# Norm weights and token factors moved from the normed tile to the copies out of PSUM, in a two-layer pooling, attention and expert kernel

## The reference, cut to what matters

```python
def rms_norm(x, g, eps=RMS_EPS):
    y = x * lax.rsqrt(jnp.mean(x * x, axis=-1, keepdims=True) + eps)
    return y * g

for i in range(2):
    h = rms_norm(x, norm_mix_g[i])
    x = x + (pool_mixer(h, pool_w, pool_scale) if i == 0 else diff_attention(h, wq, wk, wv, wo, ...))
    h = rms_norm(x, norm_ffn_g[i])
    x = x + hier_moe(h, ...)      # sum over two experts e of gate_e * ((silu(h @ w1[e]) * (h @ w3[e])) @ w2[e])
return rms_norm(x, final_g)
```

## Time and profile before

| | |
|---|---|
| median of 3 runs | 1154.34 us (1152.5 to 1156.3) |
| the profiled execution itself | 1155.02 us |
| its span | 1153.2 us |
| busy PE / PEld / DVE / ACT | 869.2 / 504.9 / 350.0 / 216.3 us |
| bytes moved by DMA | 427.74 MB |
| mean granted TensorE clock | 0.918 of full speed |
| chain that ended last | PE 43%, DMA 38%, DVE 9%, issue 7%, ACT 2% |

### The profile page before, as it was taken

The page is one execution under the profiler, slowest core; times in us unless marked ns, Lnnn a source line. Parts: engine busy times, 40 slices in busy tenths (PEclk is TensorE's granted clock), DMA queues, the critical chain, the costliest instruction groups (busy, mean ns, idle before and its releaser), DMA issues.

```text
span 1153.2 us, 19469 instructions
## 1 busy us (share of the span) xinstructions
PE 869.2 (75%) x7944; PEld 504.9 (44%) x7945; DVE 350.0 (30%) x815; ACT 216.3 (19%) x487; POOL 5.1 (0%) x15
## 2 busy tenths in 40 slices
PE   6978676667675687678999997888786666676865
PEld 4654334333443343344787564454443333333432
DVE  3533222221322222223156442331232222222223
ACT  3312112110111111111145212210111111101112
POOL 1000000000000000000000000000000000000000
PEclk9899899988998888888999989998898999889988
DMA  9989999999999999997403449999999999999992
GB/s 312 404 351 425 425 422 426 426 426 422 425 427 425 422 427 423 426 428 296 184 1 145 172 160 427 424 425 423 426 425 425 422 426 426 428 424 423 427 393 93
DMA packets 33196, 427.74 MB, mean 371 GB/s; under 512 B 4292, under 2 KB 5572, under 8 KB 7704
## 3 DMA queue, kind: packets, MB, share of 16 engines
q1 hardware_dynamic: 32600, 424.18, 87.4%
q0 software_dynamic: 448, 1.25, 0.5%
HBM read 424.37 MB, written 1.05 MB: 369 GB/s over the span
## 4 chain that ended last, share of the span: by engine, by line
PE 43%; DMA 38%; DVE 9%; issue 7%; ACT 2%; DVEq 0%; SPq 0%; ACTq 0%
DMA ring<-in_moe_w 38%; PE ps L426 15%; PE ps L462 7%; PE ps L595 5%; PE ps L477 4%; DVE work L1017 3%; PE ps L581 3%; PE ps L393 3%; PE ps L649 2%; DVE work L1025 1%; ACT work L725 1%; PE ps L379 1%; DVE hT L1051 1%; DVE work L1019 1%; DVE work L1021 1%
## 5 line engine op out<-in xcount | busy, mean ns | idle before, releaser
L426 PE MATMUL ps<-ring,work 128*32 128x256 f32 x4224 | 304.0, 439 | 193.7 <-DMA ring<-in_moe_w 114.2
L426 PEld LDWEIGHTS ps<-ring,work 128*32 128x32 f32 x4224 | 163.7, 125 | 335.1 <-issue 249.2
L1015 DVE TENSOR_SCALAR work<-work 128x128 f32<-128x128 f32 (+1 forms) x64 | 14.7, 229 | 493.3 <-ACT work L725 493.3
L393 PE MATMUL ps<-work,h_sb 128*128 128x256 f32 x576 | 150.6, 409 | 12.5 <-issue 11.8
L462 PE MATMUL ps<-ring,work 128*32 128x256 f32 x2112 | 131.3, 384 | 27.1 <-DVE work L1025 25.9
L1051 DVE COPY hT<-ps 32x512 f32<-32x512 f32 x128 | 87.4, 683 | 160.6 <-PE ps L462 159.7
L393 PEld LDWEIGHTS ps<-work,h_sb 128*128 128x128 f32 x576 | 110.1, 201 | 55.6 <-issue 42.2
L725 ACT ACTIVATE work<-ps 128x256 f32<-128x256 f32 x64 | 24.5, 383 | 502.3 <-PE ps L426 502.3
L462 PEld LDWEIGHTS ps<-ring,work 128*32 128x32 f32 x2112 | 62.8, 110 | 94.0 <-DVE work L1025 47.6
L733 ACT COPY hT<-ps 32x512 f32<-32x512 f32 x128 | 73.9, 577 | 135.7 <-PE ps L462 135.0
L477 PE MATMUL ps<-hT,work 128*128 128x512 f32 x136 | 62.6, 605 | 12.1 <-DVE hT L1051 12.1
(11 more groups left out here) (146 smaller groups left out, 421.5 us busy)
## 6 DMA issues: line engine op xcount, KB each, us to landing
ring<-in_moe_w SPq DMA_DIRECT2D x192, 2048.0 KB, 30.4
ring<-in_attn_wv SPq DMA_DIRECT2D x2, 2048.0 KB, 32.2
ring<-in_attn_wq SPq DMA_DIRECT2D x2, 2048.0 KB, 32.7
ring<-in_attn_wk SPq DMA_DIRECT2D x2, 2048.0 KB, 33.1
ring<-in_attn_wo SPq DMA_DIRECT2D x2, 2048.0 KB, 35.7
x_sb<-in_x SPq DMA_DIRECT2D x2, 512.0 KB, 6.4
work<-in_pool_w SPq DMA_DIRECT2D x1, 1024.0 KB, 13.0
out_x<-h_sb SPq DMA_DIRECT2D x2, 512.0 KB, 3.3
```

The costliest lines, as they stand in the source:

```text
L393: mm = pe.matmul(xg_ps(bank)[:, q, :], h_sb[:, t, kt * P:(kt + 1) * P], onehot[:, u, t].rearrange("p b e s -> p (b e s)"), start=(t == 0), ...
L426: mm = pe.matmul(gu_ps[SB * j:SB * (j + 1), b, :, :], xg[:, u, kt, b, k, :], w[:, :, kt, P * j:P * (j + 1)], start=(kt == 0 and b == 0), s ...
```

## The change: what it does

- h_sb, gain and root no longer stand between x and the transposes. PE transposes x_sb itself, reading every eighth element, as soon as x is there (s_x2).
- The gain of a norm, now as columns (gcol, features on partitions), multiplies in copy_hT: ACT does four products of 128x128 with a scale per partition, DVE one product with a broadcast operand. In the experts the gain comes with the copy of the gathered tokens, now two instructions of 128x256 where one of 128x512 stood.
- The root for attention: v is multiplied by it in its copies; q and k, whose tokens lie along the free axis, are multiplied by rrow, a row that PE makes by a product of ones with a diagonal matrix that DVE writes from the root. DVE now does the q and k copy, as one product of 128x512; ACT did two of 128x256.
- normalise_tokens writes h_sb permuted from x_sb times the root.
- ACT's order changes: copy_hT comes ahead of norm. In layer 0 both halves are transposed before the first router product, and both token factors come after both copies.
- Three column loads of gcol stand in SP's queue after the constants; two row loads and two broadcasts are gone. POOL's load of the second ffn gain is gone, and the one of final_g waits for s_x2 at 4.
- Three banks are cleared before the ranks and one after them, which takes the place of the extra product.
- PE's spare passes move out of experts. After layer 0 PE runs second_layer as the body of a condition "at most 64 tokens", and the spare passes with a second copy of second_layer stand in its else part; after layer 1 a branch over the spare passes stays.

```diff
-            for r, g in enumerate((norm_mix_g[0:1, :], pool_scale[0:1, :], norm_ffn_g[0:1, :], norm_mix_g[1:2, :])):
+            for r, g in enumerate((norm_mix_g[0:1, :], pool_scale[0:1, :])):
...
             sp.dma_start(cst[:, :], consts[:, 0:C_BAND]).then_inc(s_c, 16)
+            for i, g in enumerate((norm_mix_g[1, :], norm_ffn_g[0, :], norm_ffn_g[1, :])):
+                sp.dma_start(gcol[:, i, :], g.rearrange("(p k) -> p k", k=KT)).then_inc(gcol_in, 16)
...
-            def transposes(count, t):
-                pe.wait_ge(s_h, 2 * count + t + 1)
+            def transposes(number, t):
+                pe.wait_ge(s_x2, 2 * number + t + 1)
                 for k in range(KT):
                     mm = pe.transpose(ps[:, 2 * t + k // 4, (k % 4) * P:(k % 4 + 1) * P],
-                                      h_sb[:, t, k * P:(k + 1) * P], ident)
+                                      x_sb[:, t, :].rearrange("p (q k) -> p k q", k=KT)[:, k, :], ident)
...
+                if layer == 0:
+                    for t in range(TH):
+                        transposes(number, t)
                 for t in range(TH):
-                    if t > 0 and layer == 0:
-                        pe.wait_ge(s_bcc, 3)
-                    if t > 0 or layer == 0:
-                        transposes(2 * layer + 1, t)
-                    if t == 0 and layer == 0:
-                        pe.wait_ge(s_bcc, 2)
-                        broadcast(3, 2)
+                    if t > 0 and layer == 1:
+                        transposes(number, t)
...
-                for b in range(ACC):
-                    pe.matmul(ps[:, b, :], zero, cst[:, 0:512], start=True, stop=True)
+                for b in range(1, ACC):
+                    clear(b)
                 pe.wait_ge(s_A, layer + 1)
...
-                keep_clock(FILL_RANKS, 0)
+                clear(0)
...
                 if t == 1:
-                    broadcast(2, 2)
                     pe.wait_ge(s_bcc, 1)
...
+            def second_layer():
+                transposes(1, 0)
...
+                pe.wait_ge(s_diag, 1)
+                for t in range(TH):
+                    mm = pe.matmul(ps[:, 4, t * P:(t + 1) * P], ones, diag[:, t, :], start=True, stop=True)
+                mm.then_inc(s_rr, 1)
...
+                route(1, 2)
+                experts(1)
+                most = pe.value_load(cnt[0:1, NE + NGRP:NE + NGRP + 1], min_val=0, max_val=S)
+                with pe.If(most > CAP):
+                    passes(1, most)
+
+            most = pe.value_load(cnt[0:1, NE + NGRP:NE + NGRP + 1], min_val=0, max_val=S)
+            with pe.If(most < CAP + 1):
+                second_layer()
+            with pe.Else():
+                passes(0, most)
+                second_layer()
...
             def copy_hT(number, t):
                 act_e.wait_ge(s_tr, 4 * number + 2 * t + 1)
-                act_e.copy(hT[:, 0:4, t * P:(t + 1) * P], ps[:, 2 * t, :].rearrange("p (k s) -> p k s", k=4))\
-                     .then_inc(s_hT[1], 1)
+                for k in range(4):
+                    ins = act_e.mul(hT[:, k, t * P:(t + 1) * P], ps[:, 2 * t, k * P:(k + 1) * P], hT_gain(number)[:, k:k + 1])
+                ins.then_inc(s_hT[1], 1)
...
-                act_e.copy(xg[:, u, KPR * r:KPR * (r + 1)].rearrange("p k b e s -> p k (b e s)"), xg_ps(bank)).then_inc(s["xgc"], 1)
+                for q in range(KPR):
+                    kt = KPR * r + q
+                    ins = act_e.mul(xg[:, u, kt].rearrange("p b e s -> p (b e s)"), xg_ps(bank)[:, q, :],
+                                    gcol[:, 1 + layer, kt:kt + 1])
+                ins.then_inc(s["xgc"], 1)
...
-                act_e.mul(h_sb[:, t, :], h_sb[:, t, :], root_x[:, t:t + 1]).then_inc(s_hn, 1)
+                act_e.mul(h_sb[:, t, :].rearrange("p (k q) -> p k q", k=KT),
+                          x_sb[:, t, :].rearrange("p (q k) -> p k q", k=KT), root_x[:, t:t + 1]).then_inc(s_hn, 1)
...
-            def copy_queries_keys(h):
-                act_e.wait_ge(s_q, h + 1)
-                act_e.mul(qT[:, h, :], ps[:, h % 2, 0:S], HD ** -0.5)
-                act_e.copy(kT[:, h, :], ps[:, h % 2, S:2 * S]).then_inc(s_qc, 1)
...
             for t in range(TH):
+                copy_hT(2, t)
                 norm(3, t, work[:, 4096:4096 + D])
-                copy_hT(2, t)
                 normalise_tokens(1, t)
...
+            def copy_hT(number, t):
+                ve.wait_ge(s_tr, 4 * number + 2 * t + 2)
+                ve.tensor_tensor(hT[:, 4:8, t * P:(t + 1) * P], ps[:, 2 * t + 1, :].rearrange("p (k s) -> p k s", k=4),
+                                 hT_gain(number)[:, 4:8].unsqueeze(2).to_broadcast([P, 4, P]), ALU.mult).then_inc(s_hT[0], 1)
+
+            def token_factor(count, t):
+                root(count, t)
                 ve.sem_inc(s_r, 1)
...
             for t in range(TH):
                 residual(t, main["sc"], ACC * (NGRP - 1))
-                norm(2, t, gain[:, 0, :], True)
                 copy_hT(1, t)
+                token_factor(2, t)
+                ins = ve.tensor_scalar(diag[:, t, :], ident, root_x[:, t:t + 1], None, ALU.mult)
+            ins.then_inc(s_diag, 1)
...
+            def copy_queries_keys(h):
+                ve.wait_ge(s_q, h + 1)
+                ve.tensor_tensor(qk[:, :, h, :], ps[:, h % 2, :].rearrange("p (m s) -> p m s", m=2), rrow[:, :, :], ALU.mult)\
+                  .then_inc(s_qc, 1)
...
             for t in range(TH):
                 residual(t, s_wo, 0)
-                router_norm(3, t, gain[:, 1, :])
                 copy_hT(2, t)
+                token_factor(3, t)
```

More of the change, by code:

```diff
@@ L64 @@
 C_ALL = C_BAND + len(WINDOWS) * BW
-FILL_RANKS, FILL_LAST = 1, 1
+FILL_LAST = 1
 def shape_constants():
@@ L107, in build @@
         hT = sb("hT", [P, KT, S])
-        gain = sb("gain", [P, 2, D])
+        gain = sb("gain", [P, D])
+        gcol = sb("gcol", [P, 3, KT])
+        rrow = sb("rrow", [P, 2, S])
         cst = sb("cst", [P, C_BAND])
@@ L563, in _ @@
             experts(0)
-            transposes(2, 0)
-            u = CPE * NE // RING + 1
-            def matrix(c, kt):
-                return ring[:, c + kt // 4, :].rearrange("p (k n) -> p k n", k=4)[:, kt % 4, :]
-            for t in range(TH):
-                wait_hT(1, t)
-                for kt in range(KT):
-                    if t == 0 and kt % 4 == 0:
-                        pe.wait_ge(loaded[kt // 4], 16 * u)
-                    if t == 0 and kt == KT - 2:
-                        transposes(2, 1)
-                    for i in range(2):
-                        mm = pe.matmul(ps[:, 2 * t + i, :], hT[:, kt, t * P:(t + 1) * P],
-                                       matrix(0, kt)[:, 512 * i:512 * (i + 1)], start=(kt == 0), stop=(kt == KT - 1))
-                mm.then_inc(s_vp, 1)
@@ L1175, in normalise @@
                 ins.then_inc(s_os, 1)
-            for h in range(1, NH + 3):
-                if h <= NH:
+            for h in range(NH + 3):
+                if h < NH:
+                    copy_queries_keys(h)
+                if 1 <= h <= NH:
                     logits(h - 1)
```

310 lines of the change are left out of this document (154 added, 156 removed).

## The result

The kernel after takes **1139.08 us** (median of 4 runs, 1138.26 to 1141.13) against 1154.48 (4 runs, 1152.5 to 1156.3) of the kernel before on the same chip: ratio 0.987, 95% interval 0.985 to 0.989. It is faster by 15.4 us. The profiled execution took 1139.63 us for a span of 1137.8; the one before had 1155.02 for 1153.2, so the two spans differ by 15.4 as well and can be taken apart.

What follows compares the result with a forecast made beforehand. It took the weight stream as the bound in the expert loops and PE in attention; 3.2 + (4.3 + 2.7 - 0.45) + 1.7 - 2.8 = 8.65 us off the median 1154.34 gave 1145.6, range 1140.5 to 1151.5.

Steps and rivals of the forecast that it cites:

- the 2.8 us that it charged for PE's strided reads: Transposes' weight loads at v and layer 1's routing: 0.09 us more per load by DVE's factor 1.56, four sets of 8.
- The head: Start of the kernel, up to the weight stream's restart: the stream runs on 3.2 us earlier (1.0 to 5.1).
- The two waits side by side: Before the transposes between the layers: norm and PE's far branch, branch ending last by 0.5 us; removing both gains 4.3.
- The rival of a clock that stays low: At the v product between the layers: PE's clock stays low, gain 6.0 us, time 1148.3; chance 0.25.
- the branch that is only moved: Between the layers: new condition still jumps, transposes start at 522.9 as before; gain 1.6 us, 1152.7; chance 0.08.
- the rival with 0.25: Transposes' strided weight loads on PE are free: gain 11.5 us, time 1142.8; chance 0.25.
- The standstill: At the head: ring full at about 56.3 us, DMA engines start again at about 62.1, 5.8 us of standstill.
- The queued residual: Layer 1's routing: DVE's second-half residual queues behind its wait for the factor, ending at 662.1 instead of 660.46.
- the router product starts at 664.0 instead of 664.46: Layer 1's routing, after DVE's second-half residual; with the moved clear, 1.7 us together.
- The clear moved behind the ranks: Layer 1's routing: one clear of four moves behind the ranks; with the earlier router product, ranks at 672.6, 1.7 us together.
- under the stream, 0: Expert loops: 72 copies of gathered tokens become 144, about 0.1 us more each, hidden under the weight stream.
- The end and the attention loop: End: one more jump on PE, 0, at worst 0.1 us; attention: DVE takes q and k copies, 0.7 us each, cost 0.

Runs made afterwards that it cites:

- the four kernels: Kernel before; it with only PE's spare passes set aside, 1152.08 us; kernel after with them back behind the loop, 1150.54; kernel after.
- first pair: First profiled executions of the kernels before and after, cut into stretches at the same events; differences sum to 15.4 us.
- gcol_pool: Kernel after with the three column loads of the norm weights issued by POOL instead of SP: 1139.72 us.
- second pair: Both kernels, unchanged, profiled again: before 1156.34 us, after 1139.88; the differences of their stretches sum to 15.7 us.
- single edits: Kernel before with only PE's spare passes set aside, 1152.08 us; kernel after with the spare passes back behind the loop, 1150.54 us.

## Why the prediction was right, and where it was not

The forecast failed by two terms of its sum: the 2.8 us that it charged for PE's strided reads, which measured 0.02 us for each set of 8, and the 0 that it put for layer 1's expert loop, which gained 3.2. With these two as measured its sum of 8.65 would be 14.65, and the time 1139.7. The head was underrated by 1.2 to 2.0 us as well, and the routing overrated.

*Between the layers: right.* The two waits side by side, the mechanism on which the forecast rested, are what the four kernels show. The way from the scatter's end to v shrank by 4.5 us in the first pair and 4.9 in the second (4.3 was put, less 0.7 for strides), and v by 2.0 to 2.6 (2.7 for the clock, less 0.45, less 0.7). The rival of a clock that stays low is out at v, where the first 24 records took 10.54 us, and so is the branch that is only moved: 80 ns. A low clock behind a short idle did occur at layer 1's second router product, which took 3.48 us behind 0.87 us of idle time, as before the change.

*Strided reads: wrong, the step from the load to the path.* DVE's factor of 1.56 was carried to PE's weight load and every load was charged in full, -2.8 us. Measured: the load record grew by 0.05 us where 0.09 was put, and the pace of transposes by 0.002, 0.07 us for 32. The overlap was what the sum had left out. This was the rival with 0.25, and with it alone the time would have been 1142.8, which is inside the range and still 3.7 us too high.

*The head: right in kind, 3.2 for a measured 4.4 to 5.2.* Two terms of the sum were off. The ring was put 2.6 us later by three issues at 1.05 each; it started 0.7 later. The router products were put at 3.63 us for each half, 7.3 in all, the price at the low clock; all 32 records took 5.98, so the logits came 4.6 us sooner, not 3.0. The standstill went nearly whole, and gcol_pool shows no more to win there.

*Layer 1's routing: wrong.* 1.7 was put, and 0.3 after the strides; the pairs show 1.4 and -0.4, which is the clock's scatter. The queued residual was found as predicted. But the step "the router product starts at 664.0 instead of 664.46" named DVE as what comes last, and costed ACT's strided scaling as hidden behind it, at 0.6 more where it is 1.0. As soon as DVE is relieved ACT ends the wait, at the same instant. The clear moved behind the ranks gained only in the execution that the rows are from, where the clears ran at the low clock.

*The expert loops: wrong, the step "under the stream, 0".* The work inside the loop is hidden, as said; the loop's own code was not looked at. Layer 1's stream is 3.2 to 3.3 us shorter. This is half of the miss of 6.5 us, and the only part that no rival named. The split copies were put at 0.1 us more each; a pair takes 0.94 us for 0.59, hidden as forecast.

*The end and the attention loop: right.* DVE's eight products take 692 ns each and attention stays at 103.6 us; the far jump ends before the span does.

The terms again, forecast to measured: 3.2 to 4.4, 3.6 to 4.5, 1.55 to 2.0 (with 0.5 lost ahead of the scatter in the first pair), 0.3 to 1.4 or -0.4, 0 to 3.2, 0 to 0.4. The first four stand for the head, the way to v, v and the routing; then come layer 1's stream and the end. In the second pair the end is 0.9 us longer, so only the head, the way to v, v and the stream were underrated beyond what two executions differ by.

## What to carry to other kernels

Where two waits end within half a microsecond of each other, price them as a pair. Here neither edit alone shortened the way from the scatter's end to v (6.1 and 7.1 us for 6.2 or 6.6), and both together took it to 1.7 and left v's start at full clock. Read what a single edit gains by stretches, too: the 2.8 and 4.4 us of the single edits came from other places. Before charging an access pattern, measure it on the engine that will do it, and at the pace of a row of such instructions: one instruction's record can grow without costing anything. And do not read a 1.4 us gain out of a single profile. In the stretches in which TensorE ran at either clock two executions of the same kernel differed by up to 1.9 us (last gate product to v, before), while attention and the way from layer 1's first gather to its exponential came back within 0.1 in both kernels, and v in the kernel after.

## What the runs showed of the hardware

- Instructions on their way to the engines are traffic on the DMA engines: 23 further packets of about 8 KB on the queue of an idle engine lengthened a stretch of 439 us of weights by 5.9 us, 8 packets by nothing. They delayed one of the 16 parts in which a load lands, by 0.5 to 0.7 us each, and no other part.
- The 16 parts of one 2 MB load drift apart in a saturated stream: about 2 us from first to last at 36 us into layer 1's stream, and at its end eight parts land about 10 us ahead of the other eight. The last part sets when the chunk can be used, and the stream's last 10 us run at about half rate.
- Moving PE's code by 64 instructions changed its waits for instructions in the expert loops from 79.5 to 63.4 us and layer 1's stream by 1.5 to 1.9 us, with nothing else altered.
- PE's weight load from a 32-bit tile with a step of 32 bytes takes 193 ns for 141, and a row of transposes keeps its pace all the same (0.117 against 0.114 us each); ACT reads such a tile in 2.16 us for 1.15.
- The branch that jumps over the spare passes takes 3.3 to 7.1 us on PE in every profile that has it; where the body lies elsewhere it is an 80 ns compare. The Trainium skill (Runtime: NRT & Kernel Launch, section Instruction fetch mechanics) calls the fetching of straight code mostly hidden. PE's expert loops contain jumps, and there it waited 48 to 80 us for instructions, nearly all of it under the weight stream; no run here tests straight code alone.
